# A layer norm put in another order, and an inverse square root in eight steps instead of eleven

## The reference, cut to what matters

```
def rms_norm(x, g):
    y = xf * lax.rsqrt(jnp.mean(xf * xf, axis=-1, keepdims=True) + EPS)
...
def layer_norm(x, g, b):
    mu = jnp.mean(xf, axis=-1, keepdims=True)
    var = jnp.mean(jnp.square(xf - mu), axis=-1, keepdims=True)
    y = (xf - mu) * lax.rsqrt(var + EPS)
    return (y * g + b)
...
def conformer_conv(h, w_pw1, b_pw1, w_dw, b_dw, ln_g, ln_b, w_pw2, b_pw2):
    a = h @ w_pw1 + b_pw1
    g = a[..., :D_MODEL] * jax.nn.sigmoid(a[..., D_MODEL:])
    y = depthwise_conv(g, w_dw, width=31) + b_dw
    y = jax.nn.silu(layer_norm(y, ln_g, ln_b))
    return y @ w_pw2 + b_pw2
```

## Time and profile before

| | |
|---|---|
| median of 3 runs | 1654.76 us (1654.35 to 1655.68) |
| profiled execution | 1652.92 us, its span 1651.1 us |
| TensorE busy | 1611.0 us, 98% |
| VectorE busy | 930.2 us, 56% |
| ScalarE busy | 667.9 us, 40% |
| mean granted TensorE clock | 0.993 |

### The profile page before, as it was taken

The page is one execution under the profiler, slowest core; times in us unless marked ns, Lnnn a source line. Parts: engine busy times, 40 slices in busy tenths (PEclk is TensorE's granted clock), DMA queues, the critical chain, the costliest instruction groups (busy, mean ns, idle before and its releaser), DMA issues.

```text
span 1651.1 us, 26203 instructions
## 1 busy us (share of the span) xinstructions
PE 1611.0 (98%) x11087; PEld 1559.3 (94%) x11087; DVE 930.2 (56%) x1580; ACT 667.9 (40%) x1002; POOL 287.4 (17%) x343
## 2 busy tenths in 40 slices
PE   8989999999999999999999999989999999999998
PEld 6988889899999999999999999969999999999998
DVE  5556767766776644554358989967742232223232
ACT  3436545553544423432246656755432211221122
POOL 0001111000165524452342122230000000000000
PEclk9999999999999999999999999989999999999999
DMA  9322233132254434433333289873222222221211
GB/s 318 97 69 77 86 98 103 35 115 77 91 165 140 149 120 135 143 126 122 122 122 90 72 181 183 172 150 69 78 77 77 77 77 77 77 77 60 88 59 64
DMA packets 140141, 178.12 MB, mean 108 GB/s; under 512 B 12753, under 2 KB 116889, under 8 KB 139000
## 3 DMA queue, kind: packets, MB, share of 16 engines
q1 hardware_dynamic: 117824, 109.68, 20.9%
q0 software_dynamic: 21872, 66.66, 16.2%
q10 hardware_dynamic: 328, 0.10, 0.0%
HBM read 148.93 MB, written 2.79 MB: 92 GB/s over the span
## 4 chain that ended last, share of the span: by engine, by line
PE 82%; DVE 10%; DMA 3%; ACT 3%; issue 1%; POOL 0%; SPq 0%; DVEq 0%; ACTq 0%; POOLq 0%
PE PS L687 25%; PE PS L689 24%; PE PS L692 24%; DVE YACC L2295 5%; DMA ZACC<-ZTAP 2%; PE PS L757 1%; PE PS L1010 1%; PE PS L784 1%; PE PS L1021 1%; DMA Y<-SHIFT 1%; DMA XROWS<-in_x_sample 1%; PE PS L973 1%; DVE GP L2259 0%; PE PS L846 0%; DVE HL L1883 0%
## 5 line engine op out<-in xcount | busy, mean ns | idle before, releaser
L687 PE MATMUL PS<-HH,WH 128*128 128x320 f32 x1776 | 410.7, 313 | 4.8 <-DVE HL L1883 4.4
L689 PE MATMUL PS<-HL,WH 128*128 128x320 f32 x1776 | 405.1, 309 | 0.0
L692 PE MATMUL PS<-HH,WL 128*128 128x320 f32 x1776 | 403.8, 309 | 0.0
L1735 DVE TENSOR_TENSOR WL<-RAW,WH 128x2048 fp32r<-128x2048 f32 (+2 forms) x87 | 196.1, 2254 | 204.8 <-ACT WH L1271 204.7
L687 PEld LDWEIGHTS PS<-HH,WH 128*128 128x128 f32 x1776 | 296.1, 189 | 8.1 <-issue 5.7
L689 PEld LDWEIGHTS PS<-HL,WH 128*128 128x128 f32 x1776 | 298.4, 188 | 0.0
L692 PEld LDWEIGHTS PS<-HH,WL 128*128 128x128 f32 x1776 | 298.2, 189 | 0.0
L1271 ACT ACTIVATE WH<-RAW 128x2048 fp32r<-128x2048 f32 (+2 forms) x95 | 171.6, 1806 | 112.7 <-PE PS L692 112.7
L1899 DVE SCALAR_TENSOR_TENSOR X<-PS,MODV,X 128x128 f32<-128x128 f32 (+2 forms) x192 | 72.4, 434 | 198.7 <-PE PS L692 198.6
L609 POOL TENSOR_TENSOR BGACC<-BGACC,BGW 128x512 f32<-128x512 f32 x98 | 135.0, 1377 | 197.0 <-ACT BGW L1526 195.9
L687 PE MATMUL PS<-HIDH,WH 128*128 128x320 f32 x704 | 162.2, 311 | 0.7 <-DVE HIDL L2218 0.7
(11 more groups left out here) (320 smaller groups left out, 2292.4 us busy)
## 6 DMA issues: line engine op xcount, KB each, us to landing
BGW<-in_w_mod POOLq DMA_DIRECT2D x112, 256.0 KB, 3.0
RAW<-in_ffn_w_gate SPq DMA_DIRECT2D x22, 1024.0 KB, 5.3
RAW<-in_ffn_w_up SPq DMA_DIRECT2D x22, 1024.0 KB, 5.3
RAW<-in_ffn_w_down SPq DMA_DIRECT2D x16, 1024.0 KB, 5.2
MODA<-in_w_mod POOLq DMA_DIRECT2D x48, 256.0 KB, 3.8
MODS<-in_w_mod SPq DMA_DIRECT2D x16, 512.0 KB, 12.2
RAW<-in_conv_w_pw SPq DMA_DIRECT2D x16, 512.0 KB, 5.3
WL<-RAW POOLq DMA_DIRECT2D x8, 1024.0 KB, 10.3
```

Of the source, the lines that this page charges most:

```text
L687: mm(o, wh, xh, start=first, stop=False)
L689: mm(o, wh, xl, start=False, stop=False)
L692: ins = mm(o, wl, xh, start=False, stop=last)
L1735: V.tensor_tensor(WL[:, u % 2, 0:n], RAW[:, u % 2, 0:n], WH[:, u % 2, 0:n].bitcast(F32), ALU.subtract).then_inc(lo_done, 1)
```

## The change

The layer norm's steps stand in another order, and all roots have other steps.

- ScalarE makes SHIFT after 12 of the 18 tap diagonals of the last tile, and no SHIFT7; the negated copy of the pw2 unit moves behind the third square. The Silu table is loaded after OFFSET.
- POOL shifts tiles 0 to 5 only; tile 6 is shifted by VectorE ahead of the last tile's remaining taps. POOL's WL transfer comes after the OFFSET transfers.
- VectorE squares tile 7 itself and no longer adds it to SUM; a tile of sevens (SEVENS) takes SHIFT7's part.
- The sums of values have a PSUM tile of their own ("srow"), ahead of the squares' ("stat"); their rows are transposed and reduced first. TensorE adds tile 7 to the mean after the transposes and ahead of the held matmuls. EPS and the division by D move into the remaining steps.
- The root's guess is one instruction, followed by a third-order step of four and a Newton step of three.

```diff
+SHIFT_DIAGS = 12
...
-    o += [("stat", "ln"), "mu", ("turn", "ln"), ("rb", "ln")] + [("pw2", m) for m in range(KT)] + ffn(1)
+    o += ["mu", ("srow", "ln"), ("stat", "ln"), ("turn", "ln"), ("rb", "ln")] + [("pw2", m) for m in range(KT)] + ffn(1)
...
-            pool.wait_ge(sem("shift_made"), 1)
-            for i in range(KT - 1):
-                if i >= SUM_BY_DMA:
-                    was_read(pool, ("cv", i))
-                    pool.wait_ge(sem("sq_added"), NORMS["mu"] - 1)
+            was_read(pool, "shift")
+            for i in range(SUM_BY_DMA):
                 pool.dma_start(Y[:, i, :], SHIFT[:], accum_op=ALU.add).then_inc(y_shifted[i], 16)
-            unit_low(KT - 1 + LOW_BY_DMA)
             was_read(pool, "mu")
             for i in range(CENTRE_BY_DMA, KT):
...
                 pool.dma_start(Y[:, i, :], OFFSET[:], accum_op=ALU.add).then_inc(y_centred[i], 16)
+            unit_low(KT - 1 + LOW_BY_DMA)
...
-            for k in range(0, KT - 2, 2):
-                square_sums(k)
-            for i in range(2):
-                mm(mean[:, i, 0:HALF], ONES[:], SHIFT7[:, i * HALF:(i + 1) * HALF], start=True, stop=False)
+            square_sums(0)
+            square_sums(2)
+            pe.wait_ge(sem("sevens_set"), 1)
+            mean_part(SEVENS, SHIFT, True, False)
             pe.wait_ge(sem("sq_added"), NORMS["mu"])
+            mean_part(ONES, SUM, False, False).then_inc(mm_done, 1)
             for g in range(GROUPS):
-                mm(rows[COLG * g:COLG * (g + 1), 1, 0:3 * P], ONES[:, 0:COLG], (SUM, SHIFT7)[g // 2][:, halves3[g % 2]],
-                   start=True, stop=True)
+                mm(means[COLG * g:COLG * (g + 1), 0, 0:3 * P], (ONES, SEVENS)[g // 2][:, 0:COLG], (SUM, SHIFT)[g // 2][:, halves3[g % 2]],
+                   start=True, stop=g >= 2)
+            square_sums(4)
+            pe.wait_ge(sem("last_shifted"), 1)
+            for g in range(2):
+                ins = mm(means[COLG * g:COLG * (g + 1), 0, 0:3 * P], ONES[:, 0:COLG], Y[:, KT - 1, halves3[g]], start=False, stop=True)
+            ins.then_inc(mm_done, 1)
             square_sums(KT - 2).then_inc(mm_done, 1)
-            for i in range(2):
-                ins = mm(mean[:, i, 0:HALF], ONES[:], SUM[:, i * HALF:(i + 1) * HALF], start=False, stop=True)
...
-            for b in range(2):
+            for b, n in ((1, ("srow", "ln")), (0, ("stat", "ln"))):
+                was_read(pe, n)
                 for i in range(3):
                     ins = tr(ps[:, b, i * P:(i + 1) * P], LNROW[:, b, i * P:(i + 1) * P], EYE[:])
-            ins.then_inc(mm_done, 1)
+                ins.then_inc(sem("means_turned") if b else mm_done, 1)
+            mean_part(ONES, Y[:, KT - 1, :], False, True).then_inc(sem("mean_whole"), 1)
             hold_clock(rows, HOLD)
             spread(("rb", "ln"), diagn, DIAGS["ln"])
...
                     tap_diagonals(i, 0, FIRST_DIAGS)
+                    round_units(U[("glu", i)] + 2)
+                    tap_diagonals(i, FIRST_DIAGS, SHIFT_DIAGS)
+                    filled(act, "shift")
+                    A(row2(SHIFT[:]), tile2("shift")[:, :, 0:HALF], ACT.Copy, scale=-1.0 / (SUM_BY_DMA * P)).then_inc(free_of("shift"), 1)
+                    tap_diagonals(i, SHIFT_DIAGS)
+                    continue
...
+            for i in range(KT - 1):
+                act.wait_ge(y_shifted[i], 16)
                 A(LNQ[i][:], Y[:, i, :], ACT.Square).then_inc(sem("sq_made"), 1)
+                if i == 2:
+                    negated(KT - 1 + LOW_BY_DMA)
+            for b, n in ((1, ("srow", "ln")), (0, ("stat", "ln"))):
+                filled(act, n)
+                A(LNROW[:, b, :], tile2(n)[:, 0, 0:3 * P], ACT.Copy).then_inc(free_of(n), 1)
+            act.wait_ge(sem("mean_whole"), 1)
             A(row2(OFFSET[:]), tile2("mu")[:, :, 0:HALF], ACT.Copy, scale=-1.0 / D).then_inc(free_of("mu"), 1)
+            A(LNSS[:, 0:1], ONES[:, 0:1], ACT.Silu)
...
-                link(V.tensor_scalar(RSI[:, 0:n], RS[:, 0, 0:n].bitcast(I32), 1, None, ALU.arith_shift_right))
-                link(V.tensor_scalar(RS[:, 1, 0:n].bitcast(I32), RSI[:, 0:n], -1.0, 1597463007.0, ALU.mult, ALU.add))
-                for _ in range(3):
...
+                x, y, u, h = [RS[:, i, 0:n] for i in range(4)]
+                link(V.tensor_scalar(y.bitcast(I32), x.bitcast(I32), -0.5, 1597463007.0, ALU.mult, ALU.add))
+                link(V.tensor_tensor(u, y, y, ALU.mult))
+                link(V.tensor_tensor(h, u, x, ALU.mult))
+                link(V.scalar_tensor_tensor(out=u, in0=h, scalar=-10.0 / 3.0, in1=h, op0=ALU.add, op1=ALU.mult))
+                link(V.scalar_tensor_tensor(out=y, in0=u, scalar=5.0, in1=y, op0=ALU.add, op1=ALU.mult))
+                link(V.tensor_tensor(u, y, y, ALU.mult))
+                link(V.scalar_tensor_tensor(out=h, in0=u, scalar=-0.5 * 0.375 ** 3, in1=x, op0=ALU.mult, op1=ALU.mult))
+                link(V.scalar_tensor_tensor(out=y, in0=h, scalar=1.5 * 0.375, in1=y, op0=ALU.add, op1=ALU.mult))
...
                     V.tensor_tensor(SUM[:], SUM[:], Y[:, i, :], ALU.add).then_inc(sem("sq_added"), 1)
                     n_add[0] += 1
+                    V.memset(SEVENS[:], KT - 1.0).then_inc(sem("sevens_set"), 1)
+                    was_read(dve, "shift")
+                    dve.wait_ge(sem("sq_added"), n_add[0])
+                    V.tensor_tensor(Y[:, i, :], Y[:, i, :], SHIFT[:], ALU.add).then_inc(y_shifted[i], 16)
...
-            add_sum(KT - 1, None, Y[:, KT - 1, :])
+            V.tensor_tensor(LNQ[KT - 1][:], Y[:, KT - 1, :], Y[:, KT - 1, :], ALU.mult).then_inc(sem("last_squared"), 1)
...
+            dve.wait_ge(sem("means_turned"), 1)
+            link(token_sums(1))
+            link(V.scalar_tensor_tensor(out=RS[:, 2, 0:6], in0=HST[:, 6:12], scalar=1.0 / (D * D), in1=HST[:, 6:12],
+                                        op0=ALU.mult, op1=ALU.mult))
+            link(V.tensor_scalar(RS[:, 3, 0:6], RS[:, 2, 0:6], 1.0, -EPS, ALU.mult, ALU.add))
             filled(dve, n)
...
+            token_sums(0).then_inc(free_of(n), 1)
             was_read(dve, n)
...
+            for to, a, b in ((0, 0, 3), (3, 4, 6)):
+                ins = V.scalar_tensor_tensor(out=RS[:, 0, to:to + b - a], in0=HST[:, a:b], scalar=1.0 / D, in1=RS[:, 3, a:b],
+                                             op0=ALU.mult, op1=ALU.subtract)
+            link(ins)
             inverse_root()
```

More of the change, by code:

```diff
@@ L327, in program @@
         LNQ = [sb(f"LNQ{i}", [P, TOK], R_HL + i * TOK * 4) for i in range(KT)]
-        SHIFT, SHIFT7, OFFSET = [sb(n, [P, TOK], R_HH + i * TOK * 4) for i, n in enumerate(("SHIFT", "SHIFT7", "OFFSET"))]
+        SHIFT, OFFSET = [sb(n, [P, TOK], R_HH + i * TOK * 4) for i, n in enumerate(("SHIFT", "OFFSET"))]
+        SEVENS = sb("SEVENS", [P, P], R_HH + 2 * TOK * 4)
         LNROW = sb("LNROW", [P, 2, 3 * P], R_T[0])
@@ L354, in program @@
         RS = small("RS", [P, 4, 12])
-        RSI = small("RSI", [P, 12], I32)
         KPSS = small("KPSS", [P, 12])
@@ L487, in program @@
         NORMS, DIAGS, nsum, ndiag = {}, {}, 0, 0
-        for n, adds in (("ck", KVT), ("cq", QLT), ("ffn0", KT), ("mix1", KT), ("mu", KT - SUM_BY_DMA + 1), ("ffn1", KT)):
+        for n, adds in (("ck", KVT), ("cq", QLT), ("ffn0", KT), ("mix1", KT), ("mu", KT - SUM_BY_DMA), ("ffn1", KT)):
             nsum += adds - 1
@@ L494, in program @@
         SQ_BASE, nsq = {}, 0
-        for n, tiles in (("mix0", KT), ("ck", KVT), ("cq", QLT), ("ffn0", KT), ("mix1", KT), ("ln", KT), ("ffn1", KT)):
+        for n, tiles in (("mix0", KT), ("ck", KVT), ("cq", QLT), ("ffn0", KT), ("mix1", KT), ("ln", KT - 1), ("ffn1", KT)):
             SQ_BASE[n] = nsq
@@ L1214, in _ @@
             halves3 = (slice(0, 3 * P), slice(2 * P, TOK))
-            rows, mean = begin(("stat", "ln")), begin("mu")
+            mean, means, rows = begin("mu"), begin(("srow", "ln")), begin(("stat", "ln"))
             def square_sums(k):
-                pe.wait_ge(sem("sq_made"), SQ_BASE["ln"] + k + 2)
+                if k < KT - 2:
+                    pe.wait_ge(sem("sq_made"), SQ_BASE["ln"] + k + 2)
+                else:
+                    pe.wait_ge(sem("sq_made"), SQ_BASE["ln"] + KT - 1)
+                    pe.wait_ge(sem("last_squared"), 1)
                 for g in range(GROUPS):
@@ L1674, in _ @@
                 if i:
-                    tap_diagonals(i, FIRST_DIAGS if i == KT - 1 else 0)
-                    if i - 1 < SUM_BY_DMA:
-                        conv_out(i - 1)
-            filled(act, "shift")
-            for dst, tiles in ((SHIFT, 1.0), (SHIFT7, KT - 1.0)):
-                ins = A(row2(dst[:]), tile2("shift")[:, :, 0:HALF], ACT.Copy, scale=-tiles / (SUM_BY_DMA * P))
-                if dst is SHIFT:
-                    ins.then_inc(sem("shift_made"), 1)
-            ins.then_inc(free_of("shift"), 1)
-            A(HST[:, 0:1], ONES[:, 0:1], ACT.Silu)
-            for i in range(KT):
-                if i < KT - 1:
```

(16 more changed lines are left out.)

30 lines of the change are left out of this document (12 added, 18 removed).

## The result

The changed kernel took 1641.22 us in the median of 4 executions (1640.54 to 1641.64); the kernel before, on the same chip beside it, 1654.55 (4 executions, 1652.76 to 1655.68). The ratio is 0.992, with a 95% interval of 0.9904 to 0.9936: a gain of 13.3 us, 10.6 to 15.9. The profiled execution took 1641.51 us against a span of 1639.6; that span is 11.5 us shorter than before's 1651.1.

What follows compares the result with a forecast made beforehand. TensorE, busy 98% of the span, bounds the kernel, so only its waits can give time. Layer norm order 8.4 plus roots 2.4 makes 10.8 us, from a median of 1654.76 to 1644.0 us; range 1642.0 to 1648.5.

Steps and rivals of the forecast that it cites:

- The new order: Layer norm, convolution's end to pw2: earlier SHIFT and reordered steps start pw2 at 1109.0 instead of 1117.39, gaining 8.4 us.
- The held matmuls: Layer norm: twelve held pairs ahead of the spread set its start, 1.1 us after VectorE's first diagonal is there.
- POOL's queue: Behind OFFSET's six transfers, the WL transfer for pw2's second unit lands at 1121.1, hidden with 2 us to spare.
- VectorE's new wait: VectorE's wait for SHIFT ahead of ten taps: harmless if SHIFT comes by 1082.9, else taps move by the excess.
- Rivals 2, 4 and 5: 2: POOL's queue or root terms fail, 1645–1646.4 (0.15); 4: GpSimd kept from descriptors, 1654.2 (0.02); 5: late SHIFT, 1656 (0.03).
- rival 1: Layer norm: TensorE's clock falls during its sums, leaving a gain of 4.9 to 9.1, 1646 to 1650 us; chance 0.17.
- The root: All 14 roots: eight steps instead of eleven, 0.61 us off each; 2.4 us gained where TensorE or mixing 1 waits.
- heads 2, 4 and 6: Attention: three other heads waited 1.2 us together, 0.4 each, less than 0.61, so 1.2 us gained.
- Mixing 1's 0.6: Mixing 1: the root stands in VectorE's queue before the awaited background step and the whole apply; 0.6 us gained.
- Head 0's 0.6: Attention, head 0: TensorE waited 1.0 us and the chain runs through root, spread and RK; 0.6 us gained.
- 0.5 of run spread: Forecast range: the run-to-run variation allowed for in drawing 1642.0 to 1648.5 us.

Runs made afterwards that it cites:

- x7_negfirst: Changed kernel with the negated weight copy put back in front of ScalarE's tap diagonals 6 to 11 instead of behind the third square: 1644.18 us.
- x13_oldroot: `x12_best` with the old root's eleven steps in place of the eight: 1641.88 us.
- x14_best2: `x12_best` run once more, unchanged, with the new root: 1639.02 us.
- x2_order: Changed kernel with the old root, so the layer norm's new order alone: 1647.29 us.
- x1_root: Kernel before with the new root alone: 1649.5 us.
- x12_best: Changed kernel with 25 more held matmul pairs where the clock fell, 8 instead of 12 ahead of the spread, 4 ahead of the second square sums: 1639.05 us.

## Why the prediction was right, and where it failed

**The new order: right.** Forecast 8.4 us, measured 8.3 between the two profiles. SHIFT was to be made 10.2 us ahead of the convolution's end, and was, by 10.0; six transfers issued in 5.29 us, and the sixth square started 8.84 us behind the first, 1.77 a step; the seventh tile's addition hid under the ZACC wait; the spread was to start 12.35 us behind the convolution's end (1103.4 - 1091.05) and did by 12.48 (1100.27 - 1087.79). The held matmuls set that start with 0.98 us to spare, forecast 1.1, and removing them moved the spread as it had to. One small gain was put at nothing: the convolution was to resume behind the mean as before, and it did so earlier, as the diagonal was there; that is the 0.32 us of `x7_negfirst` above.

**POOL's queue and VectorE's new wait: right.** No wait for WL, by either order. SHIFT came before VectorE asked for it; where it came 3.3 us later, the taps moved and the convolution did not. Rivals 2, 4 and 5 did not come. Six transfers issued from GpSimd while VectorE did additions and its first taps went out at 0.88 us each. So the rule of the Trainium skill, page "SBUF — State Buffer", section "A bandwidth-pool intuition that's wrong (but worth ruling out)", that such a transfer waits for its descriptors during VectorE's two-port work, did not show here either. Whether these additions and taps are two-port work at all is shown by no run, so the rule itself is not refuted.

**The clock, rival 1: right for this kernel, but nearer than 0.17 made it.** In the changed kernel's two profiles the layer norm kept 2.4 GHz. With 0.7 us more of waiting it had 1.2 GHz and 1.65 us more to pay; I had priced it at 1.7 to 5.9 us, and the lower end was the right one. (The gain of 9.1 us given for it is the 10.8 less 1.7; half of 5.9 us, as the words there say, would make it 7.8.)

**The root: the term that was mis-sized.** Its own chain is as forecast: 2.22 us from its first step to the diagonals in `x13_oldroot`, 1.61 in `x14_best2`, 0.61 off. I gave heads 2, 4 and 6 "0.4 each", because 1.2 us of idle time was listed. That is 0.61 to 0.62 each by `x13_oldroot`: the whole of the three steps. The trace counts idle time from a modelled end that hides the first 0.17 us of a wait. Mixing 1's 0.6 was right (0.60). Head 0's 0.6 is right where the clock is up (0.57); where it is at 0.5, as in both of the changed kernel's profiles, TensorE itself reaches the diagonal late and no DIAGK wait is listed. Counted from the spread of norm ck, RK(0) comes after 51.31 and 51.39 us there and after 51.73 in `x2_order` with the old root, so the root gives some 0.4 us. In sum the places make it 2.8 to 3.0 us in this kernel, against 2.4. `x1_root` gained 4.3 us (2.8 to 6.0), of which the layer norm's 0.6 belongs to the old order alone.

**The sum against the range: the step that failed.** 8.3 + 0.3 + 2.8 to 3.0 makes 11.4 to 11.6 us, and the forecast had 10.8: the root's term was 0.4 to 0.6 too small, and 0.3 was left out. That alone would give 1643.2 to 1643.4 us, inside the range. The measured 13.3 has an interval of 10.6 to 15.9 and holds both sums. What put the time below the range is the step from the sum to a time, with 1654.76 us, the median of three runs, as the start and "0.5 of run spread" as the margin. Over all 9 executions of the changed kernel the mean is 1641.6 us, over 48 others of the kernel before 1654.05, from 1651.0 to 1656.95: 12.5 us, and single executions of one program differ by up to 6 us. They differ with the clock: of the 48, the five with a mean granted clock of 0.993 took 1652.1 us in the mean, the twenty with 0.992 1653.5, thirteen with 0.991 1654.4, seven with 0.990 1655.5 and three with 0.989 1656.4. The profile that I read was one of those with 0.993, so it held less low clock than most executions, and the changed kernel's have 0.993 to 0.996, with 0.994 in its profiles. The 1 us or so between 11.5 and 12.5 may be low clock of the kernel before that its one profile did not show. That is argued and not shown, since the clock's course is not known for executions without a profile. The runs of the parts speak rather against it: the order alone gained 7.8 us, no more than its stretch, and the root alone 4.3, more than its places, though the executions of `x1_root` have the mean granted clock of the kernel before, 0.991. The cause of this last us stays open; it is also within what 9 executions can tell.

## What to carry to other kernels

Where an engine's work waits on a chain of small instructions, count the whole chain's saving if the listed idle time is within some 0.2 us of it; an idle time of 0.4 us behind a matmul may be a wait of 0.6. Where work with a fixed length, such as held matmuls, stands in front of a wait, work out by how much it covers the wait before you give a shorter chain a price. And before a range is drawn from one profile, ask which stretches of low clock and which landings that one execution happened to have: here single times of one program lay up to 6 us apart, where the larger part of the change is worth 8.3.

With held pairs where the clock had fallen, `x12_best` and `x14_best2` (one kernel, 8 executions, 1637.71 to 1639.57 us) take 2 to 3 us less than the changed kernel and scatter by 2 us instead of 6.
